# Delta-rule stage: value units scaled and two late blocks evacuated by ScalarE, decay products one chunk later, third quarter of the first inversion level behind the scores

## The chip, the cores and the metric

One core of a Trainium2 chip runs the whole program in one launch. The metric is the device time of one execution in microseconds; its median was taken over three runs. Lower is better.

## The reference, cut to what matters

The program is six blocks of a small model on 256 tokens of width 1024, in ten stages: four feed-forward blocks, gated linear attention, differential attention, two pooling mixers, a gated delta rule and latent attention. The change touches the gated delta rule (`gdn_mixer`):

```python
qkv = silu(causal_depthwise_conv(qkv, conv_w))      # 4 taps, 4096 channels
q, k, v = split(qkv, [1024, 2048])                  # 8 heads; q, k of 128, v of 256
q = l2norm(q) * 128 ** -0.5;  k = l2norm(k)
beta = sigmoid(b_raw);  g = -exp(a_log) * softplus(a_raw + dt_bias)
decay = exp(where(causal, cumsum(g)_i - cumsum(g)_j, -inf))
L = where(strict, (k * beta) @ k.T * decay, 0)
sol = triangular_solve(I + L, [v * beta, k * beta * exp(g)])
attn = where(causal, q @ k.T * decay, 0)
# a recurrence over the chunks follows, then rmsnorm * silu(gate) @ w_out
```

## The kernel before, in words

Tokens lie on partitions, in two tiles (`TT`) of 128. A product with weights is cut into output blocks of 512 columns and each block into chunks of two 128-row weight tiles; the delta rule's `gdn.qkv` has 8 blocks (0 to 7) of 4 chunks (0 to 3), and "chunk (6,2)" below is chunk 2 of block 6. Each chunk is loaded by SP into one of four slots of `w_raw`, rounded by ScalarE into `w_hi` (L1439), and VectorE takes the rest into `w_lo` (L2104). TensorE then does `w_hi` with both halves of the activations (L785) and `w_lo` with the high half (L790). ScalarE may round a chunk when the slot's last one is used up by TensorE; VectorE can go on only behind that rounding. Blocks alternate between two pairs of `acc` banks, and a block is evacuated, scaled by `rstd`, before the next but one.

Each engine runs its own program in order. What stands between the chunks is written out in two tables that all engines follow: `gdn_under`, by (block, chunk behind which it comes), and `gdn_after`, for all that comes behind block 7, where the chunks are those of `gdn.gate`. The steps are:

- `conv` u: TensorE transposes unit u (256 channels, half a block; units 0 to 7 are q and k, 8 to 15 the values, one head each) into a bank of `tp` (L745). ScalarE writes the last tap (L1861, for units 12 to 15 L1886), VectorE adds the other three (L2596), ScalarE applies SiLU (L1878, L1895).
- `after_conv` u: for values, TensorE transposes the unit back into the next bank of `tp` (L745), and VectorE scales it by the key norms into `v` (L2625). The two banks of `tp` go round; `tp_ready` and `tp_free` count their fillings and releases.
- `decay` n, n = 0 to 3: one product of 512 columns into `mx` (L1195) and its exponential on ScalarE (L1916). Product n waits for the exponential of n - 2.
- `reach`: two small products (L1201, L1202), an exponential (L1920) and a negation on VectorE (L2632).
- `score` n, n = 0 to 7: four products into one bank of `mx` (L1213), which VectorE takes with the decays: even n with L2644, odd n with L2649. GpSimd then masks the attention part (L669). Product n waits until n - 2 is taken.
- `invert` q, q = 0 to 3: the first level of the block-wise inversion for a quarter of the heads and tokens: a copy under a mask (L2661) and a transpose (L2663), both on VectorE.
- `step` t: the further levels. A product into `mx` (L1220), its copy on ScalarE (L1947), a product of that into `tp` (L1220), copied under a mask by VectorE (L2672) and transposed (L2675).
- `gate` (i, p): chunk p of block i of the gate product; `evac`: the evacuation of block 7 on ScalarE (L1902). Blocks 0 to 6 are evacuated by VectorE (L2198).

## Time and profile before

| | us |
|---|---|
| median of 3 runs | 1996.28 |
| lowest, highest | 1995.08, 1999.26 |
| the profiled execution | 1994.11 |
| its span | 1992.3 |
| TensorE busy | 1920.0 |
| VectorE busy | 1212.8 |
| ScalarE busy | 988.8 |
| GpSimd busy | 65.5 |

The span runs from the first to the last instruction of the profiled execution; its own time is 1.8 us longer. The delta rule lies between about 1211 and 1490 us of the span. An engine's busy share is an average over ten stages with different limits, so the waits and the order in time of the stage are read beside it.

### The profile page before, as it was taken

What the parts mean: (1) busy time and instruction counts of PE and PEld (TensorE: products, weight loads), DVE (VectorE), ACT (ScalarE), POOL (GpSimd) and SP (SyncE); (2) the same over time, 40 slices, a digit from 0 to 9 for tenths busy, and PEclk for the clock granted to TensorE, in tenths of its full rate; (3) what the DMA queues carried; (4) which work ended last, traced back from release to release, by engine and by line L of the source; (5) the groups of instructions that cost most, each with busy time, mean ns of one, the idle gap of its engine ahead of it and who ended that gap; (6) DMA issues with size and microseconds to landing.
All of it is one profiled execution on the core that took longest, in us unless ns stands there. A gap on an engine that the chain in (4) does not pass through costs nothing.

```text
span 1992.3 us, 26363 instructions
## 1 busy us (share of the span) xinstructions
PE 1920.0 (96%) x9384; PEld 1608.9 (81%) x9384; DVE 1212.8 (61%) x1659; ACT 988.8 (50%) x1483; POOL 65.5 (3%) x95
## 2 busy tenths in 40 slices
PE   9999989999999999899999999989999999999998
PEld 7888778888788887688888887868878788878886
DVE  5555795555555568665546466887565456655554
ACT  6444665454545455654444555644365533334454
POOL 1000000000000000000000001010000021100000
PEclk9999899999999999999999999999999999999999
DMA  7655434656585554255565555432135543336453
GB/s 227 189 179 185 127 115 145 190 179 191 176 276 180 184 176 148 73 178 184 184 197 176 173 178 175 157 96 75 51 129 177 149 153 100 121 104 209 156 182 116
DMA packets 215891, 316.88 MB, mean 159 GB/s; under 512 B 16658, under 2 KB 115208, under 8 KB 215536
## 3 DMA queue, kind: packets, MB, share of 16 engines
q1 hardware_dynamic: 212704, 306.76, 48.8%
q0 software_dynamic: 3024, 8.75, 1.3%
q8 instruction: 66, 1.08, 0.2%
q14 instruction: 33, 0.27, 0.0%
q10 hardware_dynamic: 64, 0.02, 0.0%
HBM read 314.41 MB, written 3.16 MB: 159 GB/s over the span
## 4 chain that ended last, share of the span: by engine, by line
PE 86%; DVE 8%; ACT 4%; issue 2%; DMA 0%; SPq 0%; DVEq 0%; ACTq 0%
PE acc L785 49%; PE acc L790 24%; PE tp L745 3%; DVE w_lo L2104 2%; PE tp L1220 1%; PE tp L911 1%; DVE arena L2596 1%; PE mx L1220 1%; DVE arena L2349 1%; ACT w_hi L1439 1%; ACT arena L1465 1%; PE mx L1360 1%; PE mx L1361 1%; DVE x L2176 1%; PE mx L1101 1%
## 5 line engine op out<-in xcount | busy, mean ns | idle before, releaser
L2104 DVE TENSOR_TENSOR w_lo<-w_raw,w_hi 128x1024 fp32r<-128x1024 f32 (+1 forms) x589 | 713.1, 1218 | 511.9 <-ACT w_hi L1439 509.9
L1439 ACT ACTIVATE w_hi<-w_raw 128x1024 fp32r<-128x1024 f32 (+1 forms) x589 | 613.3, 1048 | 560.3 <-PE acc L790 539.2
L785 PE MATMUL acc<-w_hi,norm_hi 128*128 128x512 f32 x1488 | 474.0, 400 | 4.2 <-DVE norm_lo L2123 3.5
L785 PE MATMUL acc<-w_hi,norm_lo 128*128 128x512 f32 x1488 | 460.5, 391 | 0.0
L790 PE MATMUL acc<-w_lo,norm_hi 128*128 128x512 f32 x1488 | 397.0, 389 | 0.0
L785 PEld LDWEIGHTS acc<-w_hi,norm_lo 128*128 128x128 f32 x1488 | 280.9, 189 | 59.9
L790 PEld LDWEIGHTS acc<-w_lo,norm_hi 128*128 128x128 f32 x1488 | 279.1, 188 | 58.4
L785 PEld LDWEIGHTS acc<-w_hi,norm_hi 128*128 128x128 f32 x1488 | 273.2, 190 | 59.2 <-DVE norm_lo L2123 2.9
L785 PE MATMUL acc<-w_hi,inner_hi 128*128 128x512 f32 (+1 forms) x864 | 266.7, 390 | 6.8 <-DVE inner_lo L2123 5.3
L785 PE MATMUL acc<-w_hi,inner_lo 128*128 128x512 f32 (+1 forms) x864 | 262.4, 385 | 0.0
L790 PE MATMUL acc<-w_lo,inner_hi 128*128 128x512 f32 (+1 forms) x864 | 226.2, 383 | 0.0
L785 PEld LDWEIGHTS acc<-w_hi,inner_hi 128*128 128x128 f32 x864 | 158.6, 189 | 35.5 <-issue 6.6
L785 PEld LDWEIGHTS acc<-w_hi,inner_lo 128*128 128x128 f32 x864 | 162.2, 188 | 30.7
L790 PEld LDWEIGHTS acc<-w_lo,inner_hi 128*128 128x128 f32 x864 | 161.5, 188 | 30.3
L745 PE MATMUL tp<-ident,arena 128*128 128x128 f32 x622 | 90.3, 278 | 19.4 <-DVE inner_lo L2123 4.3
L745 PEld LDWEIGHTS tp<-ident,arena 128*128 128x128 f32 x622 | 74.1, 142 | 36.6 <-issue 15.9
L2229 DVE SCALAR_TENSOR_TENSOR arena<-acc,rstd,arena 128x256 f32<-128x256 f32 x88 | 38.6, 480 | 57.0 <-ACT arena L1555 56.9
L1555 ACT ACTIVATE arena<-acc,rstd 128x256 f32<-128x256 f32 x88 | 36.8, 470 | 63.3 <-PE acc L790 63.2
L2123 DVE SCALAR_TENSOR_TENSOR norm_lo<-tp,gains,norm_hi 128x256 fp32r<-128x256 f32 x80 | 34.0, 478 | 44.2 <-ACT norm_hi L1451 44.2
L2118 DVE TENSOR_TENSOR inner_lo<-tp,inner_hi 128x512 f32 (+1 forms) x64 | 43.8, 685 | 25.2 <-ACT inner_hi L1448 25.2
L1448 ACT ACTIVATE inner_hi<-tp 128x512 f32 (+1 forms) x64 | 38.3, 598 | 40.5 <-PE tp L911 23.1
L1451 ACT ACTIVATE norm_hi<-tp,gains 128x256 fp32r<-128x256 f32 x80 | 32.2, 471 | 32.6 <-PE tp L745 32.5
(311 smaller groups left out, 1335.7 us busy)
## 6 DMA issues: line engine op xcount, KB each, us to landing
w_raw<-in_ffn_w_gu SPq DMA_DIRECT2D x352, 256.0 KB, 3.0
w_raw<-in_ffn_w_down SPq DMA_DIRECT2D x88, 512.0 KB, 4.5
w_raw<-in_pool_w_in SPq DMA_DIRECT2D x64, 512.0 KB, 3.6
w_raw<-in_gdn_w_in SPq DMA_DIRECT2D x48, 512.0 KB, 3.8
w_raw<-in_pool_w_out SPq DMA_DIRECT2D x32, 512.0 KB, 4.3
w_raw<-in_mla_w_in SPq DMA_DIRECT2D x26, 512.0 KB, 3.7
w_raw<-in_gla_w_in SPq DMA_DIRECT2D x24, 512.0 KB, 3.6
w_raw<-in_diff_w_in SPq DMA_DIRECT2D x24, 512.0 KB, 4.3
```

What stands on the lines that cost most here:

```text
L745: last = pe.transpose(bank(tp, u, col, P), src, ident[:, :])
L785: pe.matmul(acc_of(g, i, part, tok, 0, w), t[:, tile * SEQ + tok * P:tile * SEQ + (tok + 1) * P], b_hi, start=t is hi and k + kk == 0, sto ...
L790: last = pe.matmul(acc_of(g, i, part, tok, 0, w), x_of[kk, tok], slot(w_lo, g, i, p, kk * w, w), start=False, stop=k + kk == kt - 1)
L1220: last = pe.matmul(dst[:, c * P:(c + 1) * P], gdn_t[lhs][:, cols], gdn_t[rhs][:, cols], start=True, stop=True)
L1439: act.activation(slot(w_hi, g, i, p, 0, n), slot(w_raw, g, i, p, 0, n), ACT.Copy).then_inc(S["rounded"], 1)
L1448: last = act.activation(hi[:, bass.ds(k * SEQ, BANK)], bank(tp, u), ACT.Copy)
L1451: last = act.activation(hi[:, (k + c) * SEQ:(k + c + 1) * SEQ], bank(tp, u, c * SEQ, SEQ), ACT.Copy, scale=gains[:, gain(k + c):gain(k + c ...
L1555: last = act.activation(silu[:, half + tok * SEQ:half + (tok + 1) * SEQ], acc_of(up, i, 0, tok, 0, SEQ), ACT.Silu, scale=rstd[:, tok:tok + 1])
L2104: dve.tensor_tensor(slot(w_lo, g, i, p, 0, n), slot(w_raw, g, i, p, 0, n), slot(w_hi, g, i, p, 0, n).bitcast(F32), ALU.subtract).then_inc( ...
L2118: last = dve.tensor_tensor(lo[:, bass.ds(k * SEQ, BANK)], bank(tp, u), hi[:, bass.ds(k * SEQ, BANK)].bitcast(F32), ALU.subtract)
L2123: last = dve.scalar_tensor_tensor(out=lo[:, cols], in0=bank(tp, u, c * SEQ, SEQ), scalar=gains[:, gain(k + c):gain(k + c) + 1], in1=hi[:, ...
L2229: last = dve.scalar_tensor_tensor(out=act_t[:, at_tok], in0=acc_of(up, i, 0, tok, SEQ, SEQ), scalar=rstd[:, tok:tok + 1], in1=silu[:, at_t ...
```

## The change

Four edits, all in the delta-rule stage.

1. Decay products 2 and 3 come behind chunk (6,2) instead of (6,1), and the reach step behind (6,3) instead of (6,2).
2. The third quarter of the first inversion level (`invert` 2) comes behind score 7 instead of score 5.
3. The value units are scaled by ScalarE (L1914 of the changed kernel) instead of VectorE (L2625), each as two activations from `tp`. ScalarE then releases the bank, and VectorE waits for `tp_free` before it takes a bank.
4. Block 6 is evacuated by ScalarE too (L1904), behind the last taps of units 10 and 11.

```diff
--- before.py
+++ after.py
@@ -465,14 +465,16 @@
         qkv_blocks = (2 * GDN_QK + GDN_V) // BANK
         gdn_under = {(b + 2, 2): [("after_conv", 2 * b), ("after_conv", 2 * b + 1)] for b in range(qkv_blocks - 2)}
         gdn_under.setdefault((qkv_blocks - 2, 0), []).extend([("decay", 0), ("decay", 1)])
-        gdn_under.setdefault((qkv_blocks - 2, 1), []).extend([("decay", 2), ("decay", 3)])
-        gdn_under.setdefault((qkv_blocks - 2, 2), []).append(("reach", 0))
+        gdn_under.setdefault((qkv_blocks - 2, 2), []).extend([("decay", 2), ("decay", 3)])
+        gdn_under.setdefault((qkv_blocks - 2, 3), []).append(("reach", 0))
         for q in range(3):
-            gdn_under.setdefault((qkv_blocks - 1, 1 + q), []).extend([("score", 2 * q), ("score", 2 * q + 1), ("invert", q)])
+            gdn_under.setdefault((qkv_blocks - 1, 1 + q), []).extend([("score", 2 * q), ("score", 2 * q + 1)])
+        for q in range(2):
+            gdn_under[qkv_blocks - 1, 1 + q].append(("invert", q))
 
 
         last = 2 * qkv_blocks - 4
-        gdn_after = [("score", 6), ("score", 7), ("invert", 3), ("conv", last), ("conv", last + 1), ("evac", 0), ("gate", (0, 0)),
+        gdn_after = [("score", 6), ("score", 7), ("invert", 2), ("invert", 3), ("conv", last), ("conv", last + 1), ("evac", 0), ("gate", (0, 0)),
                      ("silu", last), ("silu", last + 1), ("gate", (0, 1)), ("after_conv", last), ("step", 0), ("step", 1),
                      ("conv", last + 2), ("gate", (0, 2)), ("after_conv", last + 1), ("step", 2), ("step", 3), ("silu", last + 2),
                      ("conv", last + 3), ("gate", (0, 3)), ("after_conv", last + 2), ("step", 4), ("step", 5), ("silu", last + 3),
@@ -1894,18 +1896,27 @@
                     act.wait_ge(S["tp_free"], 2 + tapped[u])
                     see["gdn_conv_done"].up(act.activation(conv[:, cols], conv[:, cols], ACT.Silu))
 
-                def evac_last(_):
-
-                    wait_evacuated(act, qkv_g, blocks - 2)
-                    wait_block(act, qkv_g, blocks - 1)
+                def evac_late(i):
+
+                    wait_evacuated(act, qkv_g, i - 1)
+                    wait_block(act, qkv_g, i)
                     for tok in range(TT):
-                        last = act.activation(gdn_t["block"][:, tok * BANK:(tok + 1) * BANK], acc_of(qkv_g, blocks - 1, 0, tok), ACT.Copy,
+                        last = act.activation(gdn_t["block"][:, tok * BANK:(tok + 1) * BANK], acc_of(qkv_g, i, 0, tok), ACT.Copy,
                                               scale=rstd[:, tok:tok + 1])
                     last.then_inc(S["dve_evac"], 1)
 
                 def after_conv(u):
                     if u >= 2 * qk_blocks:
-                        plain_units(1)
+                        h = u - 2 * qk_blocks
+                        see["tp_ready"].take(act)
+                        for tok in range(TT):
+                            n = tok * GDN_H + h
+                            last = act.activation(gdn_t["v"][:, n * GDN_DV:(n + 1) * GDN_DV],
+                                                  bank(tp, (see["tp_ready"].n - 1) % 2, tok * SEQ, GDN_DV), ACT.Copy,
+                                                  scale=gdn_t["norms"][:, TT * GDN_H + n:TT * GDN_H + n + 1])
+                            if tok == 0:
+                                act.wait_ge(S["tp_free"], 2 + see["tp_ready"].n - 1)
+                        last.then_inc(S["tp_free"], 1)
                     elif u == 2 * qk_blocks - 1:
                         see["gdn_ssq_ready"].take(act, u + 1)
                         see["gdn_norms_ready"].up(act.activation(gdn_t["norms"], mx[:, 0:2 * TT * GDN_H], ACT.Sqrt, bias=eps[:, :]))
@@ -1952,15 +1963,19 @@
                 def after(u):
                     after_conv(u)
                     conv_read[u] = see["tp_ready"].n
-                steps = dict(after_conv=after, decay=decay, reach=reach, score=lambda n: None, evac=evac_last, invert=lambda n: None,
+                steps = dict(after_conv=after, decay=decay, reach=reach, score=lambda n: None, evac=lambda n: evac_late(blocks - 1), invert=lambda n: None,
                              conv=tap_last, silu=silu, step=step_of, gate=gate_chunk)
                 for i in range(1, blocks):
                     for p in range(qkv_g.n):
                         feed.to(qkv_g.chunk(i, p) + 1 + HEAD)
                         for name, n in gdn_under.get((i, p), []):
                             steps[name](n)
+                    def between_taps():
+                        if i == blocks - 2:
+                            evac_late(i)
+                        feed.before_evac(qkv_g, i, ahead=SLOTS)
                     if i < blocks - 1:
-                        convolve([2 * i - 2, 2 * i - 1], lambda: feed.before_evac(qkv_g, i, ahead=SLOTS))
+                        convolve([2 * i - 2, 2 * i - 1], between_taps)
                 for name, n in gdn_after:
                     steps[name](n)
                 plain_units(2)
@@ -2586,6 +2601,7 @@
 
                     see["turned_hi"].take(dve)
                     see["tp_ready"].n += 1
+                    see["tp_free"].wait(dve)
                     for k in range(GDN_CONV - 2, -1, -1):
                         back = GDN_CONV - 1 - k
                         if back > 1:
@@ -2618,13 +2634,8 @@
                                                                  ALU.mult))
                     if u < 2 * qk_blocks:
                         return
-                    h = u - 2 * qk_blocks
-                    see["tp_ready"].take(dve)
-                    for tok in range(TT):
-                        n = tok * GDN_H + h
-                        last = dve.tensor_scalar(v[:, n * GDN_DV:(n + 1) * GDN_DV], bank(tp, unit(), tok * SEQ, GDN_DV),
-                                                 norms[:, of_tokens + n:of_tokens + n + 1], None, ALU.mult)
-                    see["tp_free"].up(last)
+                    see["tp_ready"].n += 1
+                    see["tp_free"].n += 1
                 reach, neg_in = gdn_t["reach"], gdn_t["neg_in"]
 
                 def reached(_):
@@ -2668,6 +2679,7 @@
                     n, q = gdn_step(t - 2)
                     for name in gdn_products_of(n):
                         see["tp_ready"].take(dve)
+                        see["tp_free"].wait(dve)
                         mask = four_of((3 + n) * P if name == "inv" else (3 + LEVELS + n - 5) * P)
                         see["tp_free"].up(dve.copy_predicated(heads(part(name, q)), mask.bitcast(U32), heads(bank(tp, unit()))))
                     if 2 << n <= SQUARE:
@@ -2688,7 +2700,8 @@
                         convolve(2 * i - 2)
                         feed.before_evac(qkv_g, i, ahead=SLOTS)
                         convolve(2 * i - 1)
-                        scaled_evac(qkv_g, i, block_t, BANK)
+                        if i < blocks - 2:
+                            scaled_evac(qkv_g, i, block_t, BANK)
                 for name, n in gdn_after:
                     steps[name](n)
```

How the instructions stand. Line numbers of the changed kernel are higher by 2 on TensorE, and by 2 to 16 on the others.

TensorE, from the last products of chunk (6,1) before and (6,2) now (`L1195`/`L1197` decay, `L1201`/`L1203` reach, `tp<-ident` the transposes of units 8 and 9). Before:

```order
L790 MATMUL acc<-w_lo,norm_hi 128x512 x4
L1195 MATMUL mx<-arena,stage_const 128x512 x2
L785 MATMUL acc<-w_hi,norm_hi 128x512 x2
L785 MATMUL acc<-w_hi,norm_lo 128x512 x2
L785 MATMUL acc<-w_hi,norm_hi 128x512 x2
L785 MATMUL acc<-w_hi,norm_lo 128x512 x2
L790 MATMUL acc<-w_lo,norm_hi 128x512 x4
L745 MATMUL tp<-ident,arena 128x128 x8
L1201 MATMUL mx<-stage_const 128x8
L1202 MATMUL mx<-stage_const 128x8
```

Now:

```order
L792 MATMUL acc<-w_lo,norm_hi 128x512 x4
L747 MATMUL tp<-ident,arena 128x128 x8
L1197 MATMUL mx<-arena,stage_const 128x512 x2
L787 MATMUL acc<-w_hi,norm_hi 128x512 x2
L787 MATMUL acc<-w_hi,norm_lo 128x512 x2
L787 MATMUL acc<-w_hi,norm_hi 128x512 x2
L787 MATMUL acc<-w_hi,norm_lo 128x512 x2
L792 MATMUL acc<-w_lo,norm_hi 128x512 x4
L1203 MATMUL mx<-stage_const 128x8
L1204 MATMUL mx<-stage_const 128x8
```

The two decay products stand behind the transposes of units 8 and 9, and the reach products behind another chunk.

VectorE, from the place behind the rounding that follows inversion 0 (`mx` with `x4` and the `TENSOR_TENSOR` behind it are a pair of scores, the mask copy and transpose behind them an inversion). The first row before is the value scaling of units 10 and 11. Before:

```order
L2625 TENSOR_SCALAR arena<-tp,stage_const 128x256 x4
L2644 SCALAR_TENSOR_TENSOR arena<-mx,stage_const,arena 128x128 x4
L2649 TENSOR_TENSOR arena<-mx,arena 128x512
L2661 COPY_PREDICATED arena<-stage_const,arena 128x512
L2663 STREAM_TRANSPOSE arena<-arena 128x512
L2104 TENSOR_TENSOR w_lo<-w_raw,w_hi 128x1024
L2644 SCALAR_TENSOR_TENSOR arena<-mx,stage_const,arena 128x128 x4
L2649 TENSOR_TENSOR arena<-mx,arena 128x512
L2661 COPY_PREDICATED arena<-stage_const,arena 128x512
L2663 STREAM_TRANSPOSE arena<-arena 128x512
L2644 SCALAR_TENSOR_TENSOR arena<-mx,stage_const,arena 128x128 x4
L2649 TENSOR_TENSOR arena<-mx,arena 128x512
```

Now, from the same place:

```order
L2655 SCALAR_TENSOR_TENSOR arena<-mx,stage_const,arena 128x128 x4
L2660 TENSOR_TENSOR arena<-mx,arena 128x512
L2672 COPY_PREDICATED arena<-stage_const,arena 128x512
L2674 STREAM_TRANSPOSE arena<-arena 128x512
L2119 TENSOR_TENSOR w_lo<-w_raw,w_hi 128x1024
L2655 SCALAR_TENSOR_TENSOR arena<-mx,stage_const,arena 128x128 x4
L2660 TENSOR_TENSOR arena<-mx,arena 128x512
L2655 SCALAR_TENSOR_TENSOR arena<-mx,stage_const,arena 128x128 x4
L2660 TENSOR_TENSOR arena<-mx,arena 128x512
L2672 COPY_PREDICATED arena<-stage_const,arena 128x512
L2674 STREAM_TRANSPOSE arena<-arena 128x512
L2672 COPY_PREDICATED arena<-stage_const,arena 128x512
```

The value scaling is gone from the top, and the inversion between scores 5 and 6 has moved behind score 7, where two of them follow each other.

ScalarE, behind the evacuation of block 7 (`L1895`/`L1897` SiLU, `L1947`/`L1958` copies of step products, `L1886`/`L1888` taps of unit 14). Before:

```order
L1439 ACTIVATE w_hi<-w_raw 128x1024
L1895 ACTIVATE arena<-arena 128x512 x2
L1439 ACTIVATE w_hi<-w_raw 128x1024
L1947 ACTIVATE arena<-mx 128x512 x2
L1886 ACTIVATE arena<-tp,gains 128x256 x2
L1439 ACTIVATE w_hi<-w_raw 128x1024
```

Now:

```order
L1904 ACTIVATE arena<-acc,rstd 128x512 x2
L1441 ACTIVATE w_hi<-w_raw 128x1024
L1897 ACTIVATE arena<-arena 128x512 x2
L1441 ACTIVATE w_hi<-w_raw 128x1024
L1914 ACTIVATE arena<-tp,stage_const 128x256 x2
L1958 ACTIVATE arena<-mx 128x512 x2
L1888 ACTIVATE arena<-tp,gains 128x256 x2
```

The scaling of unit 12 (`L1914`) stands ahead of the two copies and of the taps of unit 14.

## Rows read from the trace of the kernel before

**Rows 1.** The page's first part: busy us, share of the span, instructions.
```profile
PE 1920.0 (96%) x9384; PEld 1608.9 (81%) x9384; DVE 1212.8 (61%) x1659; ACT 988.8 (50%) x1483; POOL 65.5 (3%) x95
```

**Rows 2.** Waits of TensorE, 1210 to 1495 us: total, times, longest.
```profile
PE mx L1213 <- DVE arena L2644: 5.1, 2, 2.7
PE mx L1195 <- ACT arena L1916: 2.3, 1, 2.3
PE tp L1220 <- DVE arena L2596: 1.9, 2, 1.1
...
PE tp L745 <- DVE arena L2649: 0.8, 1, 0.8
```

**Rows 3.** The chain in order of time, 1296 to 1362 us: start, us, what.
```profile
1301.05 1.28 ACT L1916
...
1302.99 1.98 PE mx L1195 x4
...
1307.73 0.87 PE tp L745 x8
...
1308.95 1.94 PE acc L785 x8
1310.90 0.91 PE acc L790 x4
...
1320.14 1.05 ACT w_hi L1439
...
1322.36 1.13 DVE arena L2644 x4
...
1328.10 1.57 DVE arena L2625 x4
```

**Rows 4.** TensorE's timeline: start, us, operation, count, idle before and releaser.
```profile
283.83 3.09 PE L1014 MATMUL mx<-arena 128*128 128x128 f32 x16 [3.35 <-DVE arena L2359]
...
1311.65 1.03 PE L745 MATMUL tp<-ident,arena 128*128 128x128 f32 x8
...
1330.75 2.05 PE L1213 MATMUL mx<-arena 128*128 128x128 f32 x16 [2.41 <-DVE arena L2644]
1335.54 3.50 PE L1213 MATMUL mx<-arena 128*128 128x128 f32 x16 [2.73 <-DVE arena L2644]
...
1353.07 1.13 PE L1220 MATMUL tp<-arena 128*128 128x128 f32 x8 [0.81 <-DVE arena L2596]
```

**Rows 5.** VectorE's timeline, 1283 to 1360 us, same columns.
```profile
1319.49 1.40 DVE L2198 TENSOR_SCALAR arena<-acc,rstd 128x512 f32<-128x512 f32 x2
...
1324.38 1.86 DVE L2661 COPY_PREDICATED arena<-stage_const,arena 128x512 f32<-128x512 uint32 x1
...
1331.53 0.75 DVE L2661 COPY_PREDICATED arena<-stage_const,arena 128x512 f32<-128x512 uint32 x1
...
1341.39 5.28 DVE L2596 SCALAR_TENSOR_TENSOR arena<-tp,gains,arena 128x255 f32<-128x255 f32 x12
...
1349.46 0.87 DVE L2625 TENSOR_SCALAR arena<-tp,stage_const 128x256 f32<-128x256 f32 x2
1350.25 2.67 DVE L2596 SCALAR_TENSOR_TENSOR arena<-tp,gains,arena 128x255 f32<-128x255 f32 x6
```

**Rows 6.** ScalarE's timeline, 1283 to 1360 us, same columns.
```profile
1341.96 1.28 ACT L1902 ACTIVATE arena<-acc,rstd 128x512 f32<-128x512 f32 x2
...
1349.16 0.83 ACT L1886 ACTIVATE arena<-tp,gains 128x256 f32<-128x256 f32 x2
```

**Rows 7.** GpSimd's timeline, 1200 to 1420 us, same columns.
```profile
1324.36 1.26 POOL L669 TENSOR_TENSOR arena<-arena,stage_const 128x512 f32<-128x512 f32 x1 [89.52 <-DVE arena L2649]
...
1336.36 1.79 POOL L669 TENSOR_TENSOR arena<-arena,stage_const 128x512 f32<-128x512 f32 x1 [2.99 <-DVE arena L2649]
```

**Rows 8.** Two stretches: length; PE, PEld, DVE, ACT, POOL busy; PEclk, DMA, GB/s.
```profile
286.00:288.00 2.00, 2.00 (x9) 1.71 (x8) 2.00 (x2) 1.97 (x3) 0.00 (x0) 0.51 0.61 170
...
1336.00:1338.00 2.00, 2.00 (x12) 2.00 (x11) 1.93 (x5) 0.00 (x0) 1.64 (x1) 0.50 0.73 247
```

## The prediction

> **What bounds the kernel now.** I read the busy shares first: TensorE is busy for 1920.0 of 1992.3 us [rows 1], so the whole kernel can give back only some 70 us, and this change touches one stage of ten. Second the waits of TensorE in the delta-rule stage [rows 2]: about 10 us, of which 5.1 us are score products waiting for VectorE (L2644), 2.3 us a decay product waiting for an exponential on ScalarE (L1916), 1.9 us products of the inversion waiting for the convolution taps (L2596), 0.8 us a transpose waiting for the last score. Third the chain in order of time through that place [rows 3], to see what the waits hang on: an activation table load, the decay products at 1302.99, then taps of unit 10 on ScalarE, a rounding L1439 at 1320.14, and from 1322.36 on VectorE nearly without a break, scores, value scaling and masks one after the other. Between 1328 and 1340 us VectorE is the bound and TensorE the waiting engine: it sat idle 2.41 and then 2.73 us [rows 4].
>
> Below, "shift" is how much earlier an event comes than in the profiled execution, which took 1994.11 us around its span of 1992.3. That is 2.2 us under the median of the runs, 1996.28; I take the same difference for the changed kernel.
>
> **Decay products one chunk later.** Products 2 and 3 waited 2.28 us of the 2.3 in [rows 2] for the exponentials of 0 and 1, which begin behind the table load of 1301.05 and end at about 1303.4 [rows 3]. Now chunk (6,2) (1.94 + 0.91 us in the chain, 2.7 behind another chunk) and the transposes of units 8 and 9 (0.87 us) come first, so TensorE, through with chunk (6,1) at about 1300.6, is at the products at about 1304.1 and waits for nothing. Their own exponentials come behind the four value scalings of units 8 and 9 on ScalarE and end near 1307.9; the reach product, a chunk later too, is asked for at 1308.6. The transposes of units 10 and 11, at 1311.65 before [rows 4], come 2.6 us earlier: 2.28, and 0.3 for a wait counted between an end and a start where products otherwise overlap, and for one break in the row of products less. Bounds 2.3 and 2.6; I take 2.6, from the starts.
>
> **Two evacuations on ScalarE.** VectorE loses its evacuation of block 6, 1.40 us at 1319.49 [rows 5]. ScalarE gains it, at the 1.28 us of its evacuation of block 7 [rows 6], between the taps of units 10 and 11 and the rounding of chunk (7,3). That rounding now ends 0.2 us after VectorE is through with unit 10, so unit 11 is 0.2 us later. The 1.40 us are not gained: behind unit 11 VectorE needs the next rounded chunk, which ScalarE rounds only after SiLU 11 (1320.14 in [rows 3]), so VectorE waits about 1.6 us where it evacuated. The first score (1322.36) shifts by 2.6 - 0.2 = 2.4 us.
>
> **Value units on ScalarE.** Units 10 and 11 stood on VectorE between score pairs, 1.57 us in the chain [rows 3]; they go, so the shift from score 2 on is 4.0 us. On ScalarE they meet an engine that waited there for a transpose, and cost nothing. Units 8 and 9 were ahead of an idle stretch of VectorE and give nothing. Here the Trainium skill, page "ScalarE: Activation LUTs", section "Rules for kernel authors", speaks against the change: it gives multiplications to VectorE. The rows show the same price for two 128x256 tiles out of PSUM in float32, 0.87 us on VectorE (L2625, [rows 5]) and 0.83 us on ScalarE (L1886, [rows 6]), so I take 0.83; by the page's factor of up to 3, stated for bf16, a unit would cost 2.5 us and the shift below would end at an estimated 1.2 instead of 2.9.
>
> **Third quarter behind the scores.** All four inversions still come before unit 12's taps on VectorE, so their sum doesn't change. Score 6's product no longer waits for inversion 2, but it still needs score 4 taken by VectorE, which comes some 3 us after TensorE has finished score 5: a wait of 3.0 us takes the place of the 2.41 and 2.73, and VectorE then waits 0.25 us for it. Against that stand 0.3 us that VectorE lost before to score 7, slow in a group of 3.50 us [rows 4]. Net nothing. But the two masks now stand 1.4 us apart behind the last scores, where GpSimd's triangle multiplication of the last scores runs. In [rows 5] the mask copy took 1.86 us at 1324.38 and 0.75 at 1331.53; the long one started 0.02 us after a GpSimd multiplication of 1.26 us [rows 7], the short one before one, and then it was GpSimd's that took 1.79, as at 1336.36 [rows 7]. So the second of two close mask copies finds GpSimd in possession and waits 0.4 us. (The Trainium skill, page "SBUF — State Buffer", says of VectorE and GpSimd that the one which starts first has the shared port pair for its whole instruction; by that rule, the trace agrees, and without it the cost would be 0.) Unit 12's taps on VectorE, at 1341.39 [rows 5], shift by 4.0 - 0.4 - 0.1 = 3.5 us.
>
> **What is late next.** TensorE itself starts the first gate chunk 5.3 us earlier, but it doesn't keep that. Its product at 1353.07 waited 0.81 us [rows 4] for the tap sums of unit 14 on VectorE, which began at 1350.25 [rows 5], the moment that VectorE was free and 0.26 us after ScalarE's taps were there (1349.16 + 0.83, [rows 6]). In the changed order ScalarE has, behind SiLU 13 and a rounding, the value scaling of unit 12 ahead of the two copies of step products and these taps: 0.8 us later. VectorE loses 0.87 us there but then waits for ScalarE. So the shift falls by 0.8 - 0.26 = 0.55, to 2.9 us, and TensorE idles about 3 us instead of 0.81. Units 13, 14 and 15 fall into waits of ScalarE of over 1 us before the next step product, with the two banks freed in time; I cost them at nothing, at most 0.8 each if that cover is gone. The waits added on VectorE (`tp_free`) are for units long done; at most 0.1 us for the two back-to-back units. No DMA is moved: SP's and GpSimd's queues are unchanged.
>
> **The clock.** The new waits are long ones. After the 2.73 us, with 2.41 us shortly before, the granted clock was 0.50 from 1336 to 1338, that is 1.2 GHz; after an isolated 3.35 us at 283.83 it was 0.51 [rows 4, 8]. After the 2.28 and after the 2.41 us it stayed at 2.4. At half clock scores 6 and 7 (a group of 3.50 us; the group before took 2.05, [rows 4]) would put 0 to 1.2 us on VectorE's chain; I take 0.8, since the clock fell some 0.4 us after the products began again. The second new wait, 3 us and isolated, lies between the rows: below nothing is excluded, the upper end is half of some 3.4 us at half clock, 1.7. I take 0, with the other case as a rival.
>
> **Sum.** 2.6 - 0.2 + 1.6 - 0.4 - 0.1 - 0.55 = 2.9 us, less 0.8 for the clock: 2.1 us. From 1994.11 that gives 1992.0 for a profiled execution, and from the median 1994.2 us. About 0.2% (4.0 us) is what a measurement of this kernel can tell from no change, so I forecast no difference to be told, on the fast side.
>
> **Rivals.**
> Half clock twice: the wait before the product of 1353.07 is followed by half clock too, -2.1 + 1.7 = -0.4 us, 1995.9. For it: 3 us is nearer to the 3.35 that was followed by it than to 2.41. Against: the products before are dense for 10 us. Chance 0.22.
> TensorE keeps its lead of 5.3 us, 1991.0: if the tap sums of unit 14 aren't what holds 1353.07, because ScalarE is through sooner than I chain it. For it only that ScalarE is busy half of the time; against it the row of 0.81 us itself. Chance 0.13.
> ScalarE becomes the bound: the four late units at 0.8 us each and the evacuation before the taps stand ahead of what TensorE waits for. -2.9 + 3 x 0.8 gives -0.5, with the clock +0.3, 1996.6. Against it are the idle times of over 1 us ahead of each step copy. Chance 0.08.
> Slower: the clock, once at 1.2 GHz behind the second wait, stays there through the small products of steps 2 to 10, about 20 us of TensorE work. It costs 10 us, -2.1 + 10 = +8, 2004. It decides once the clock is low for more than 12 us. Nothing in the stage shows so long a stretch; 0.04.
> The change doesn't do what it says: the decay wait only moves to the reach product and unit 10 stays where it was, 0 us, 1996.3. The order of instructions speaks against it; 0.03.
> My own forecast, with or without the first clock loss, has the rest, 0.50.
>
> **Numbers.** Faster by over 0.2%: the second rival and a tail of the forecast, 0.16. Slower: the fourth and little else, 0.04. Same 0.80. The range reaches from the second rival's 1991.0 to a little over the third's 1996.6, with the runs' own spread of a microsecond: 1990.7 to 1997.5.
>
> **What would show it.** In the profile of the changed kernel: no idle time before the decay products; the transposes of units 10 and 11 near 1309.0; the first score on VectorE near 1320; TensorE idle about 3.0 us once between the score pairs, not 2.41 and 2.73; one mask copy of about 1.2 us besides the first of 1.86; the first gate chunk 4 to 5 us earlier; and 3 us idle before the first inversion products out of tp, with the tap sums of unit 14 as the releaser. If that last wait is under 1 us I am wrong about what is late next; if it is 3 us and the clock after it 0.5, the first rival holds.

## The result, and the profile after

The changed kernel takes **1990.41 us** (median of 14 executions, 1983.84 to 1994.89), beside 1994.86 for the kernel before on the same chip (14 executions, 1989.22 to 1999.26). The ratio is 0.9973, interval 0.9960 to 0.9986, so it is 5.4 us faster, between 2.8 and 8.0 (the means are 5.4 us apart, the medians 4.45). The forecast was 1994.2 us, with a range down to 1990.7: direction right, size too small, the time 0.3 us outside the range. One part of that is the base: the median of 1996.28 that the forecast started from was of three executions; with 14 it is 1.4 us lower. "Faster by over 0.2%", which is what came, had been given a chance of 0.16.

The profiled execution took 1994.89 us (span 1993.1), the longest of the 14, so its span tells nothing of the gain. Within the stage it can be read all the same, if times are counted from one event ahead of it. I take the last transposes of the input x ahead of the projection, 1211.23 us before and 1211.60 after; the second is 0.37 us late, and "lead" below is with that taken out. First TensorE on the changed kernel, order of time (start, duration, operation; in brackets the idle time before and its releaser):

```profile
1303.64 1.03 PE L747 MATMUL tp<-ident,arena 128*128 128x128 f32 x8
1304.51 1.88 PE L1197 MATMUL mx<-arena,stage_const 128*128 128x512 f32 x4
...
1309.34 1.07 PE L747 MATMUL tp<-ident,arena 128*128 128x128 f32 x8
...
1327.17 2.05 PE L1215 MATMUL mx<-arena 128*128 128x128 f32 x16 [0.86 <-DVE arena L2655]
1331.96 3.09 PE L1215 MATMUL mx<-arena 128*128 128x128 f32 x16 [2.74 <-DVE arena L2655]
1335.84 1.97 PE L747 MATMUL tp<-ident,arena 128*128 128x128 f32 x8 [0.79 <-DVE arena L2660]
...
1351.27 1.13 PE L1222 MATMUL tp<-arena 128*128 128x128 f32 x8 [1.26 <-DVE arena L2612]
```

The decay products stand behind a chunk and two units' transposes and wait for nothing; the wait of 2.28 us in [rows 2] is gone. The transposes of units 10 and 11 have a lead of 1311.65 + 0.37 - 1309.34 = 2.68 us. Of the two waits of 2.41 and 2.73 us in [rows 4] the first is 0.86 now, the second 2.74. The first inversion product, 1353.07 before, has a lead of 2.17 us; the sum of the prediction said 2.1. Now VectorE over the same stretch:

```profile
1319.18 1.23 DVE L2119 TENSOR_TENSOR w_lo<-w_raw,w_hi 128x1024 fp32r<-128x1024 f32 x1 [1.65 <-ACT w_hi L1441]
1320.33 1.12 DVE L2655 SCALAR_TENSOR_TENSOR arena<-mx,stage_const,arena 128x128 f32<-128x128 f32 x4
...
1322.34 1.88 DVE L2672 COPY_PREDICATED arena<-stage_const,arena 128x512 f32<-128x512 uint32 x1
...
1333.38 1.12 DVE L2655 SCALAR_TENSOR_TENSOR arena<-mx,stage_const,arena 128x128 f32<-128x128 f32 x4 [0.68 <-PE mx L1215]
1335.09 0.69 DVE L2660 TENSOR_TENSOR arena<-mx,arena 128x512 f32<-128x512 f32 x1 [0.58 <-PE mx L1215]
1335.81 0.75 DVE L2672 COPY_PREDICATED arena<-stage_const,arena 128x512 f32<-128x512 uint32 x1
1336.60 0.71 DVE L2674 STREAM_TRANSPOSE arena<-arena 128x512 f32<-128x512 f32 x1
1337.24 1.03 DVE L2672 COPY_PREDICATED arena<-stage_const,arena 128x512 f32<-128x512 uint32 x1
1338.30 0.71 DVE L2674 STREAM_TRANSPOSE arena<-arena 128x512 f32<-128x512 f32 x1
1338.93 5.43 DVE L2612 SCALAR_TENSOR_TENSOR arena<-tp,gains,arena 128x255 f32<-128x255 f32 x12
...
1348.43 2.69 DVE L2612 SCALAR_TENSOR_TENSOR arena<-tp,gains,arena 128x255 f32<-128x255 f32 x6 [1.21 <-ACT arena L1888]
```

These answer to [rows 5]. Where VectorE evacuated block 6 it idles 1.65 us. The two mask copies behind the last scores stand 1.43 us apart, and the second takes 1.03 instead of 0.75 us: GpSimd's multiplication has begun 0.05 us after the first:

```profile
1335.86 1.80 POOL L671 TENSOR_TENSOR arena<-arena,stage_const 128x512 f32<-128x512 f32 x1 [1.80 <-DVE arena L2660]
```

VectorE's copy of the last pair of scores and the addition behind it each waited for TensorE, 0.68 and 0.58 us, because TensorE was at half clock. In fill_both below, at full clock, 0.46 us of the first wait is still there and the second is not. The granted clock is the third column from the right (1.00 is 2.4 GHz):

```profile
1330.00:1332.00 2.00, 0.04 (x1) 0.04 (x1) 1.91 (x5) 0.00 (x0) 0.00 (x0) 1.00 0.00 0
1332.00:1334.00 2.00, 2.00 (x13) 2.00 (x14) 1.31 (x4) 0.00 (x0) 1.22 (x1) 0.69 0.86 247
1334.00:1336.00 2.00, 1.22 (x6) 0.92 (x6) 1.39 (x4) 0.00 (x0) 0.20 (x2) 0.50 0.04 15
1336.00:1338.00 2.00, 2.00 (x9) 1.93 (x10) 1.97 (x3) 1.00 (x3) 1.66 (x1) 0.50 0.00 0
1338.00:1340.00 2.00, 2.00 (x7) 1.60 (x6) 1.93 (x5) 2.00 (x5) 0.00 (x0) 0.61 0.00 0
```

Before, about 3.4 us of this stretch were at 1.2 GHz (0.50 from 1336 to 1338 [rows 8], 0.68 to 1340); now it is about 6.8. Such stretches (1.2 GHz for about 3.4 us) of about 3.4 us come up all over the program, and each costs TensorE 1.7 us of work at full clock. ScalarE behind it, in the place of [rows 6]:

```profile
1338.57 1.27 ACT L1904 ACTIVATE arena<-acc,rstd 128x512 f32<-128x512 f32 x2
...
1345.88 0.82 ACT L1914 ACTIVATE arena<-tp,stage_const 128x256 f32<-128x256 f32 x2
1346.59 1.08 ACT L1958 ACTIVATE arena<-mx 128x512 f32<-128x512 f32 x2
1347.54 0.86 ACT L1888 ACTIVATE arena<-tp,gains 128x256 f32<-128x256 f32 x2
```

The value scaling of unit 12 (L1914) stands ahead of unit 14's taps (L1888), for which VectorE waits 1.21 us and then TensorE 1.26. So within the stage the order of things is the forecast one, and the gain is 2.2 us. What is not in the stage is the other half of the 4.4 to 5.4 us between the totals.

TensorE starts the first gate chunk at 1337.45, 1340.67 before: 3.6 us of lead there (5.0 in fill_both, at full clock), of which 2.2 are left at the inversion product.

### The profile page after: what moved, and what is told of

Its sections match the earlier page's. It is cut to its first block, busy times and chain, and to the rows that moved or that the text cites. A ratio compares the mean times of both kernels' runs of the same rounds, so it can differ in the third digit from the quotient of the medians.

```text
span 1993.1 us, 26408 instructions
## 1 busy us (share of the span) xinstructions
PE 1924.4 (97%) x9384; PEld 1613.5 (81%) x9384; DVE 1205.9 (61%) x1641; ACT 996.5 (50%) x1501; POOL 64.9 (3%) x95
## 4 chain that ended last, share of the span: by engine, by line
PE 86%; DVE 7%; ACT 4%; issue 2%; DMA 0%; SPq 0%; DVEq 0%; ACTq 0%
PE acc L787 50%; PE acc L792 24%; PE tp L747 3%; DVE w_lo L2119 2%; PE tp L1222 1%; PE tp L913 1%; PE mx L1222 1%; DVE arena L2612 1%; ACT w_hi L1441 1%; PE mx L1362 1%; DVE arena L2364 1%; PE mx L1363 1%; ACT arena L1467 1%; DVE x L2191 1%; PE mx L1103 1%
```

## The experiments

"First product" is the time from the last transposes of x to the first inversion product, "first score" that to the first score on VectorE, "unit 12" that to VectorE's taps of unit 12. "Profile" stands for the one profiled execution of a run. Intervals of a ratio are of 12 executions (5 of after_b, 11 of before_b, 14 of the first comparison) against 14 to 35 of the kernel before on the same chip.

**Both kernels again, and the first part alone.** decay_only is the kernel before with this much of the diff:

```
-        gdn_under.setdefault((qkv_blocks - 2, 1), []).extend([("decay", 2), ("decay", 3)])
-        gdn_under.setdefault((qkv_blocks - 2, 2), []).append(("reach", 0))
+        gdn_under.setdefault((qkv_blocks - 2, 2), []).extend([("decay", 2), ("decay", 3)])
+        gdn_under.setdefault((qkv_blocks - 2, 3), []).append(("reach", 0))
```

before_again:

> The kernel before, unchanged, timed as if it were a new one. Both theories: ratio 1.000, within 0.15%. Its trace shows how much one and the same program differs from profile to profile. Clock theory: the stage from 1211 us to the first inversion product out of tp is within 1 us of the trace before, but other stretches at half clock fall elsewhere, so that the span differs by several us with a mean granted clock that differs in the third digit. Rival: the span stays within 1 us of 1992.3.

after_again:

> The changed kernel, unchanged. Theory A (the order of work alone, without the clock, gives 2.9 us, and the measured 5.4 us is partly the luck of where half clock fell in the runs): 2 to 3.5 us faster than before. Theory B (the change removes some 5 us in every execution): 5 us or more faster. In the stage the first inversion product out of tp comes 2.0 to 2.9 us earlier, counted from the first transposes at 1211, by A; over 4 by B.

decay_only:

> Kernel before with the first edit alone: decay products and reach one chunk later. Theory A: the transposes of units 10 and 11 come 2.4 to 2.6 us earlier, the first score on VectorE also 2.4 to 2.6 earlier, and since VectorE is the bound from there, the whole comes out 2.5 us faster less what the clock does. Rival (the decay edit is swallowed by VectorE's queue): under 1 us faster.

| kernel | ratio, interval | first score | unit 12 | first product |
|---|---|---|---|---|
| before | 1 | 111.13 | 130.16 | 141.84 |
| before_again | 0.9999, 0.9987 to 1.0010 | 111.11 | 130.15 | 141.81 |
| after | 0.9973, 0.9960 to 0.9986 | 108.73 | 127.33 | 139.67 |
| after_again | 0.9978, 0.9965 to 0.9991 | 108.72 | 126.89 | 139.22 |
| decay_only | 0.9979, 0.9968 to 0.9991 | 108.49 | 127.68 | 139.35 |

The stage repeats to 0.5 us (0.6 over the four profiles of the changed kernel, two of which come below). The decay edit alone brings the first product 2.5 us earlier, all that the whole change brings (2.2 and 2.6 here, 2.0 to 2.6 over the four). The other edits add 0.35 and 0.8 us at unit 12 in these two profiles and lose it by the first product. The totals say the same: on one chip decay_only has 0.9979 and the changed kernel 0.9978. So what the totals give beyond the stage comes with the decay edit alone too.

**Filled waits.** fill_both is the changed kernel with products whose result nobody reads ahead of score 4 (3), score 6 (11) and the first inversion product (5), so that TensorE waits less with nothing to do; fill_before the kernel before with 8 ahead of score 4 and 9 ahead of score 6. late_low_fill, below, has the first two of fill_both.

```
+                    for _ in range(times):
+                        pe.matmul(acc_of(gate_g, i, 0, 0), norm_hi[:, 0:P], norm_hi[:, 0:BANK], start=True, stop=True)
```

fill_both:

> Changed kernel, with throw-away products on TensorE in its three new waits (3 before score 4, 11 before score 6, 5 before the first inversion product out of tp; they write an acc bank that the next block overwrites), so that it stays at 2.4 GHz there. Clock theory: no half clock between 1325 and 1356 us, scores 6 and 7 take 2.05 us as a group instead of 3.09, the first inversion product comes 0.8 us earlier than in the changed kernel, and the whole is 0.8 to 2 us faster than the changed kernel. Rival (half clock there is hidden by waits): no difference.

fill_before:

> The kernel before with throw-away products in TensorE's waits ahead of score 4 (8) and score 6 (9), so that the 3.4 us at half clock behind them should not come. Theory (the half clock puts about 0.5 to 1.2 us on VectorE's chain): first inversion product 140.6 to 141.4 us after the transposes of x, against 141.84 and 141.81. Rival (VectorE's chain does not see TensorE's clock there): 141.7 to 141.9, no difference. Total: theory 1993.5 to 1994.5, rival 1994.5.

In fill_both the clock was 1.00 throughout the scores, the first product came at 139.05 and the ratio was 0.9971 (0.9958 to 0.9984). In fill_before the clock was 1.00 too, and the first product came at 141.66: 0.2 us under the mean of four profiles of the kernel before (141.86), not the 0.5 to 1.2 expected, with a ratio of 0.9992 (0.9982 to 1.0003). So the half clock of the kernel before cost its chain next to nothing; in the changed kernel it costs 0.6 us (139.61, the mean of its four profiles, against 139.05). The forecast had taken 0.8 off. With the clock out of the way on both sides the change brings the first product 2.6 us earlier (141.66 against 139.05); the sum without its clock term was 2.9.

**Single parts put back.** In unit12_back VectorE scales unit 12, in values_back all eight value units, in evac_back it evacuates block 6, and invert_back has the third quarter ahead of score 6; the rest is the changed kernel.

```
+        by_vector = (12,)
...
+                        if u in by_vector:
+                            plain_units(1)
+                            return
...
```

```
-                        if i == blocks - 2:
-                            evac_late(i)
...
-                        if i < blocks - 2:
-                            scaled_evac(qkv_g, i, block_t, BANK)
+                        scaled_evac(qkv_g, i, block_t, BANK)
```

```
-        for q in range(2):
+        for q in range(3):
             gdn_under[qkv_blocks - 1, 1 + q].append(("invert", q))
...
-        gdn_after = [("score", 6), ("score", 7), ("invert", 2), ("invert", 3), ("conv", last), ...
+        gdn_after = [("score", 6), ("score", 7), ("invert", 3), ("conv", last), ...
```

unit12_back:

> The changed kernel, with unit 12's value scaling alone put back on VectorE (0.87 us there, in its idle 1.21 us ahead of unit 14's tap sums); ScalarE is 0.8 us sooner at the taps of unit 14. Times from the last transposes of x ahead of the stage (1211.23 us before, 1211.60 after) to the first inversion product: 141.8 before, 139.7 and 139.2 in two looks at the changed kernel. Theory (unit 12 on ScalarE ahead of unit 14's taps gives back 0.55 us): 138.8 to 139.2, the wait of that product on VectorE shorter by 0.3 to 0.6. Rival (VectorE is the later one there anyway): no earlier than 139.2, the wait as before. Total: within 1 us of the changed kernel's 1991.

values_back:

> The changed kernel with the value scaling of all eight units back on VectorE. Theory of the prediction: 4.0 - 0.4 us of lead at unit 12's taps fall to about 2.0 (units 10 and 11 stand between score pairs again, 1.6 us), the 0.55 us at unit 14 are not lost, so the first inversion product comes 140.0 to 140.6 us after the transposes of x, against 139.7 and 139.2 in the changed kernel. Rival (what is gained there is hidden by TensorE's half clock and unit 14 anyway, as decay_only with its 139.35 suggests): 139.2 to 139.7. Total within 1.5 us of 1991.

evac_back:

> The changed kernel with block 6 evacuated by VectorE again. Theory (the move costs 0.2 us: ScalarE's rounding comes 0.2 us later, and VectorE waits where it evacuated): first score on VectorE 108.5 us after the transposes of x (108.73 with the move, 108.49 with the decay edit alone), first inversion product 0.2 us earlier than in the changed kernel. Rival (the move frees VectorE): first score later than 108.9. Total within 1 us of 1991.

invert_back:

> The changed kernel, with the third quarter's inversion ahead of score 6 again. Theory of the prediction (net nothing but 0.4 us for the second of two close mask copies): first inversion product 139.0 to 139.7 after the transposes of x (139.7 and 139.2 with the edit), one mask copy of 1.9 us and none near 1.0. TensorE's wait ahead of score 6 may grow by the mask copy and transposition, 1.5 us, to some 4 us, with half clock behind it. Rival (score 6 then waits for VectorE longer and this delays the chain): later by 0.5 us or more. Total within 1.5 us of the changed kernel's 1991.

| kernel | ratio, interval | first score | unit 12 | first product |
|---|---|---|---|---|
| unit12_back | 0.9982, 0.9971 to 0.9992 | 108.73 | 127.17 | 139.20 |
| values_back | 0.9986, 0.9974 to 0.9999 | 108.72 | 129.60 | 141.62 |
| evac_back | 0.9992, 0.9984 to 1.0001 | 108.48 | 126.41 | 138.74 |
| invert_back | 0.9971, 0.9959 to 0.9983 | 108.74 | 126.50 | 139.32 |

unit12_back: from unit 12's taps to the first product it takes 12.03 us, where the changed kernel has 12.34 and 12.33 and the kernel before 11.68 and 11.66. So the changed kernel loses 0.66 us on this stretch, near the 0.55 of the prediction, but the unit on ScalarE is 0.3 of it. Of the other 0.35, VectorE's twelve taps make 0.15 (5.43 us against 5.28); the rest stays open. evac_back: the first score is 0.25 us sooner, so the evacuation on ScalarE costs the 0.2 us worked out and frees nothing. The rest of its lower first product is the clock's doing, which did not fall at the scores: with the 0.25 added back, 138.74 is the 139.05 of fill_both within 0.1 us.

values_back missed both expectations: 141.62, as in the kernel before. VectorE shows why:

```profile
1320.90 1.85 DVE L2647 TENSOR_SCALAR arena<-tp,stage_const 128x256 f32<-128x256 f32 x4
...
1330.76 1.12 DVE L2669 SCALAR_TENSOR_TENSOR arena<-mx,stage_const,arena 128x128 f32<-128x128 f32 x4 [1.38 <-PE mx L1216]
1332.26 0.69 DVE L2674 TENSOR_TENSOR arena<-mx,arena 128x512 f32<-128x512 f32 x1 [0.38 <-PE mx L1216]
...
1334.40 1.05 DVE L2686 COPY_PREDICATED arena<-stage_const,arena 128x512 f32<-128x512 uint32 x1
```

decay_only at the same place, with the value units on VectorE as well, but the third quarter's inversion still between the pairs:

```profile
1331.57 0.74 DVE L2661 COPY_PREDICATED arena<-stage_const,arena 128x512 f32<-128x512 uint32 x1
1332.35 0.71 DVE L2663 STREAM_TRANSPOSE arena<-arena 128x512 f32<-128x512 f32 x1
1332.98 1.08 DVE L2644 SCALAR_TENSOR_TENSOR arena<-mx,stage_const,arena 128x128 f32<-128x128 f32 x4
1334.50 0.69 DVE L2649 TENSOR_TENSOR arena<-mx,arena 128x512 f32<-128x512 f32 x1 [0.43 <-PE mx L1213]
```

Ahead of the last pair VectorE waits for TensorE in any case; decay_only does the inversion in that time, and values_back waits 1.38 us and has the inversion, with the slow second mask, still to come. How long the wait is depends on the clock: values_back and decay_only were at half clock from score 4 on, the changed kernel from score 6 on, and in fill_both, at full clock, it is 0.46 us:

```profile
1331.42 1.13 DVE L2664 SCALAR_TENSOR_TENSOR arena<-mx,stage_const,arena 128x128 f32<-128x128 f32 x4 [0.46 <-PE mx L1223]
```

So of the 2.3 us that values_back loses at unit 12 against the changed kernel (129.60, mean of four 127.28) some 1.8 are the value scaling itself and 0.5 the clock (1.38 + 0.38 of waits against 0.68 + 0.58).

invert_back says the same of the third quarter: unit 12 at 126.50, sooner than in any profile of the changed kernel (126.89 to 127.50). Moving the third quarter loses 0.4 to 1.0 us there (the prediction: 0.4, the mask alone). At the first product nothing of it can be told any more: 139.32 lies within the four profiles. So beside the moved third quarter the value move is worth about 2 us (values_back), beside the unmoved one next to nothing: invert_back's unit 12 is 1.2 us ahead of that of decay_only, its first product (139.32 against 139.35) level.

**VectorE's chain shortened.** late_low has unit 12 back on VectorE, and moves VectorE's rounding of gate chunk (0,2) and inversion 3 behind the taps of units 12 and 13. late_low_fill adds the filling products.

```
-                        feed.to(qkv_g.chunk(i, p) + 1 + HEAD)
+                        if (i, p) != (blocks - 1, qkv_g.n - 1):
+                            feed.to(qkv_g.chunk(i, p) + 1 + HEAD)
...
-        ... ("score", 7), ("invert", 2), ("invert", 3), ("conv", last), ("conv", last + 1), ...
+        ... ("score", 7), ("invert", 2), ("conv", last), ("conv", last + 1), ("invert", 3), ...
```

late_low:

> The changed kernel with unit 12 back on VectorE, and VectorE's rounding of gate chunk (0,2), 1.5 us ahead of score 4, and inversion 3, some 1.7 us, moved behind the taps of units 12 and 13, where VectorE idles 0.5 and 1.2 us. Theory (VectorE alone sets the end of the score stretch): taps of unit 12 on VectorE start 2.5 to 3.2 us earlier than in the changed kernel (127.3 and 126.9 us after the transposes of x), and the first inversion product comes 1 to 2 us earlier, 137.5 to 138.5. Rival (what is moved only lands ahead of unit 14's tap sums): first product no earlier than 138.8. Total: theory 1989 to 1990, rival 1991.

late_low_fill:

> The same with throw-away products in TensorE's waits ahead of score 4 (3) and score 6 (11), so that TensorE's clock stays at 2.4 GHz there. Theory: the clock of 1332 to 1340 us is 1.00 and the first inversion product comes another 0.2 to 0.8 us earlier. Rival: with VectorE's rounding gone, TensorE is no longer waiting 3 us, and the filling delays the scores by up to 1 us. Total: theory 1988.5 to 1989.5, rival 1990 to 1991.

late_low has unit 12 at 123.48 and the first product at 137.41, 1.8 to 2.4 us sooner than the changed kernel and a little more than theory had it (137.5 to 138.5); its ratio is 0.9973 (0.9961 to 0.9986), no better than that of the change. late_low_fill has 138.42, later by the 1 us that its rival gave to the filling, and 0.9988 (0.9978 to 0.9999). The stage of late_low shows one place where the gain goes. TensorE:

```profile
1342.39 0.63 PE L748 MATMUL tp<-ident,arena 128*128 128x128 f32 x4 [1.41 <-DVE arena L2647]
1345.18 1.62 PE L1223 MATMUL tp<-arena 128*128 128x128 f32 x8 [2.16 <-DVE arena L2616]
1346.59 1.91 PE L1223 MATMUL mx<-arena 128*128 128x128 f32 x8
```

and its clock from the windows:

```profile
1344.00:1346.00 2.00, 0.82 (x6) 0.85 (x7) 1.97 (x4) 0.47 (x1) 0.00 (x0) 0.91 0.81 271
1346.00:1348.00 2.00, 2.00 (x11) 2.00 (x11) 1.30 (x3) 0.00 (x0) 0.00 (x0) 0.50 0.36 75
```

The longer wait for unit 14 is followed by half clock: of the lead of 4.4 us over the kernel before at the first product 3.1 are left 60 us on. This is the mechanism of the first rival, in a kernel that waits there longer than the changed one does.

**The other 2 us.** after_delayed is the changed kernel with 15 filling products ahead of the first inversion product. Then both kernels once more, two copies each on one chip.

after_delayed:

> The changed kernel with 15 throw-away products of TensorE (about 0.25 us each) ahead of the first inversion product, which fill its wait of 1.26 us and go on for 2.4 us more: everything behind the stage comes at the times of the kernel before again. The runs so far put the changed kernel 4.4 to 5.4 us under the one before, the stage only 2.2 to 2.7 us. Theory (the rest comes of where TensorE's half-clock stretches behind the stage fall, and so goes with the shift): no faster than the kernel before, 1993.5 to 1995. Rival (the rest comes of the changed instructions themselves, wherever they stand in time): 2.4 us above the changed kernel, about 1993, and a total under that of before by 1.5 to 2.5 us.

before_b:

> The kernel before, unchanged, as a kernel under test. Theory 1 (the change is worth what the stage shows, 2.2 to 2.8 us, and the 4.4 to 5.4 us of the totals are chance in where the half-clock stretches fell, and in how a kernel under test stands to the comparison runs): mean of the times of before_b and before_c 2.2 to 2.8 us above that of after_b and after_c, 24 executions each. Theory 2 (some 2 us come from elsewhere): 4.2 to 5 us above. A standard error of about 0.8 us is to be expected of the difference. Against the comparison runs the ratio should be 1 within 0.0015.

after_b:

> The changed kernel, unchanged. See before_b for the two theories on the totals. In the profile: first inversion product 139.2 to 139.7 us after the transposes of x, half clock for about 6.8 us from the third wait of the scores on, and two to six further half-clock stretches behind the stage whose number decides the span.

before_c:

> The kernel before again. In the profile: first inversion product 141.8 us after the transposes of x, 3.4 us at half clock behind the waits of 2.4 and 2.7 us.

after_c:

> The changed kernel again; with after_b and the two copies of the kernel before it gives 24 executions of each on one chip, and two more profiles of each, in which the stretches ahead of the stage (the same program in both) can be compared.

| kernel | executions | mean, us | standard error | first product |
|---|---|---|---|---|
| before_b, before_c | 23 | 1993.5 | 0.6 | 141.76, 142.02 |
| after_b, after_c | 17 | 1989.1 | 0.8 | 139.83, 139.73 |
| with before_again | 35 | 1993.7 | 0.5 | 141.86 (mean of 4, with before) |
| with after, after_again | 43 | 1989.7 | 0.5 | 139.61 (mean of 4) |
| after_delayed | 12 | 1992.2 | 1.1 | 141.71 |

after_b gave only 5 executions. The difference of the means is 4.4 us (standard error 1.0) in this set and 4.0 (0.7) over all; the stage's is 2.25. That leaves 1.8 with an error of 0.7: theory 1, that nothing is left, is unlikely but not excluded. The kernel before also ran 148 times as the comparison of the other runs, at a mean of 1994.7; with these, 183 executions in all, the difference is 4.8 (0.5). The ratios say the same: 0.9998 (0.9988 to 1.0008) and 0.9999 (0.9990 to 1.0008) for the copies of the kernel before, 0.9968 (0.9955 to 0.9980) and 0.9972 (0.9961 to 0.9982) for the changed kernel. after_delayed lost 2.5 us by its delay of 2.1 and still stood 1.5 (error 1.2) under the kernel before, ratio 0.9986 (0.9975 to 0.9998), though what follows the stage began at the times of before. Beside the kernel before on its own chip (mean 1994.6) it is 2.4 (1.2). That speaks against the shift being the source of the rest, within its error.

Each execution comes with its mean granted clock, and the rest seems to lie there. A straight line through the 35 times of the kernel before gives 1.7 us for each 0.001 of the clock, through the 43 of the changed kernel 1.7 as well. At the same clock of 0.990 the lines stand 3.4 us apart; the changed kernel has one more stretch at half clock in its stage, worth 1.7 us (two in each of its four profiles, one in three of the kernel before; before_c has two as well, not the 3.4 us that was expected of it). So at an equal clock it must have one less elsewhere: 2.25 + 1.7 = 3.9, beside the 3.4 (error 0.3). And the mean clocks are 0.9902 before and 0.9906 after (errors 0.0002 each), where the added stretch alone would have made it 0.9893: by this reckoning half clock fell less often outside the stage, by 0.0013, or 2.2 us at 1.7. This is inferred from means, not seen in a trace.

Which stretches these are stays open, and the profiles show the opposite. In those of the two kernels half clock comes at eight places: near 212, 284, 778, 820, 1333, 1550, 1755 to 1766 and the end, each once, twice, three times in a row or not at all, in two profiles of one kernel too. Outside the stage, and without the end, the four of the kernel before have 9, 8, 9 and 6 stretches, the four of the changed kernel 12, 10, 9 and 11. From the transposes of x to the end of the span it is 781.1, 779.8, 780.0 and 781.0 us before, and 781.5, 778.1, 778.7 and 781.5 after: two of four keep most of the stage's lead, two lose all of it. The changed kernel near 1550, behind a wait of 3.64 us, in four windows of 2 us:

```profile
1548.00:1550.00 2.00, 1.73 (x7) 1.28 (x8) 1.00 (x3) 0.61 (x3) 0.00 (x0) 0.50 0.55 202
1550.00:1552.00 2.00, 2.00 (x5) 1.54 (x6) 1.67 (x6) 1.21 (x2) 0.10 (x1) 0.50 0.00 0
1552.00:1554.00 2.00, 2.00 (x6) 1.59 (x5) 0.88 (x1) 0.00 (x0) 2.00 (x4) 0.50 0.00 0
1554.00:1556.00 2.00, 2.00 (x8) 1.54 (x8) 0.00 (x0) 0.90 (x1) 1.30 (x4) 0.85 0.87 254
```

and after_again, the same kernel:

```profile
1548.00:1550.00 2.00, 0.82 (x4) 0.43 (x4) 1.66 (x4) 0.94 (x3) 0.00 (x0) 0.88 0.85 250
1550.00:1552.00 2.00, 1.96 (x6) 1.58 (x7) 1.10 (x4) 1.78 (x3) 0.00 (x0) 0.50 0.03 12
1552.00:1554.00 2.00, 2.00 (x9) 1.59 (x8) 1.45 (x3) 0.00 (x0) 1.49 (x2) 0.76 0.00 0
1554.00:1556.00 2.00, 2.00 (x10) 1.66 (x9) 0.20 (x1) 1.06 (x1) 1.92 (x5) 1.00 0.64 130
```

The first lost 1.2 us there against the kernel before, the second nothing. Four of the eight places lie ahead of the stage, where both kernels run the same program, so that a cause in the change is hard to see for those. Of the 43 executions of the changed kernel 11 took under 1987.5 us, of 183 of the kernel before none; no profiled execution of the changed kernel (1992.75 to 1994.89, all above its mean of 1989.7) was among them, so no trace shows what they lack.

## Why the prediction was right and wrong

- **Bounds and chain.** Right: TensorE waits for VectorE through the scores; the stage gave 2.25 us where 2.1 were forecast. That it is so near is in part luck: from the scores on the terms below are off by up to 0.6 us each, in both directions.
- **Decay products, 2.6 us.** Measured 2.68 at the transposes of units 10 and 11, and 2.4 at the first score, as 2.6 - 0.2 had it. The step is right. It was also nearly the whole of the stage's gain, which the sum did not say: it had the value scaling as +1.6 beside it.
- **Evacuation, -0.2.** Right: 0.25 in evac_back.
- **Value scaling, +1.6.** Right where it was read: the products of scores 4 and 5 come 3.95 us earlier (115.57 against 119.52), for the 4.0 of the prediction. As a term of the sum at the first product wrong. Without it and with the third quarter moved the first product comes 2 us later; without it and with the third quarter left, as in decay_only, no later at all. The two edits don't add up.
- **Third quarter, "net nothing" and -0.4 for the second mask.** The mask's price was 0.3 (1.03 against 0.75), by the mechanism named. "Net nothing" failed: "All four inversions still come before unit 12's taps on VectorE, so their sum doesn't change" is true, but the inversion had filled a wait for TensorE ahead of the last pair. The prediction put this wait at 0.25 us and set 0.3 against it; it is 0.46 at full clock (fill_both), and 0.68 with 0.58 behind it at half clock. By invert_back, 0.4 to 1.0 us at unit 12 together with the mask.
- **What is late next, -0.55.** Right in place and kind: 0.66 from unit 12 to the first product, 0.3 of it unit 12's scaling by unit12_back. The wait for unit 14 was 0.8 to 1.35 us in the four profiles, not 3, because TensorE at half clock was itself late with the gate chunk; where it kept full clock, it is the 3 us of the prediction: 2.91 in evac_back, and in fill_both 1.74 behind filling products of 1.39. The prediction named a wait under 1 us as the sign of being wrong here; the 0.82 us of after_again is under it, with the mechanism in place all the same.
- **The clock, -0.8.** It fell behind a wait of 2.74 us as forecast, for twice as long. fill_both puts its price at 0.6 us, fill_before at 0.2 in the kernel before, so the difference between the kernels is nearer to 0.4.
- **The rivals.** Half clock behind the second wait did not come in any of the four profiles of the changed kernel; it came in late_low, late_low_fill, values_back and evac_back, with waits of 2.16, 2.16, 2.16 and 2.91 us. The second rival's 1991.0 is near the measured time, but not for its reason: TensorE had 3.6 us of lead at the gate chunk, not 5.3, and the tap sums of unit 14 did hold the inversion product.
- **The failed step** is the last one, from stage to total: "I take the same difference for the changed kernel", and "the runs' own spread of a microsecond" in the range. The spread is 2.5 us and more to either side (the standard deviation is 2.6 before and 3.3 after), it goes with the granted clock at 1.7 us for each 0.001, its mean need not be the same in the two kernels, and the base from three executions was itself 1.4 us high. The 2.2 us by which the profiled execution lay under the median were nothing to carry over: those of the changed kernel lie 1.7 to 5.6 us above their medians. These make the 3.8 us between forecast and result: 1.4 for the base, 0.15 for the stage, the rest (2.2) what lies outside the stage, the clock there and chance, which the runs don't part. Its cause stays open.

## What to carry to other kernels

Undo the parts of a change one at a time: here one moved step was worth all of the stage's gain, and two others only cancelled each other, because a step moved out of a wait frees nothing and must be paid behind it. What an edit gives is what is left of it at the end of the stage, not where it is first seen: 3.95 us at scores 4 and 5 were 2.25 at the first product. Where the clock falls now and then in stretches that cost 1.7 us each, a gain of 2 us in one stage can be read from that stage's times against a fixed event in two profiles, and from totals only with some 40 executions; the spans of single profiles show it even less (here they were longer after the change than before, on average). Take a range for the total from the spread of many executions, not of three.

## What was not expected of the hardware

- Equal waits are not followed by equal clocks. evac_back waited 0.84 and 2.73 us ahead of the same scores as the changed kernel (0.86 and 2.74) and stayed at full clock; TensorE before it in the program was the same:

```profile
1320.60 2.05 PE L1215 MATMUL mx<-arena 128*128 128x128 f32 x16 [0.84 <-DVE arena L2653]
1325.38 2.05 PE L1215 MATMUL mx<-arena 128*128 128x128 f32 x16 [2.73 <-DVE arena L2653]
1328.55 1.09 PE L747 MATMUL tp<-ident,arena 128*128 128x128 f32 x8 [1.12 <-DVE arena L2658]
```

  A group of score products took 2.05 us there and 3.09 in the changed kernel. decay_only fell already behind 2.41 us. Behind the same wait the kernel before did not fall in three of its profiles, and did in before_c (the other three have 2.05 us for this group):

```profile
1325.96 2.66 PE L1213 MATMUL mx<-arena 128*128 128x128 f32 x16 [2.40 <-DVE arena L2644]
```

  What else decides, these runs don't show.
- The stage's start itself, 1211.2 us into the kernel before, lay between 1205.3 and 1212.9 us in the profiles of kernels that are the same up to there, roughly in step with the number of half-clock stretches ahead of it: 1205.3 to 1207.8 with four, 1209.1 to 1212.8 with seven, 1211.6 to 1212.9 with eight.
- Scaling two 128x256 tiles out of PSUM in float32 took 0.82 us on ScalarE (L1914) and 0.87 on VectorE (unit12_back), so in this type and size the choice of the engine is one of who is waited for.
